# Output projections that end by pairs of token tiles, the next norm's transpositions between their last steps, the first gate diagonal built first, and the odd layer's channel norm two attention units earlier

## Chip, cores and metric

One core of one Trainium2 chip. The metric is the device time of one execution in microseconds (us); lower is better. Three executions of the kernel before gave 1838.09 to 1843.55, median 1841.16.

## What is computed

Two layers of a hybrid trunk over 512 latent tokens and 256 context tokens, width 1024, in float32 precision. Each layer is: norm, mixer, norm and gated residual, norm, gated ConvFFN, norm and gated residual.

```python
for layer in range(2):
    h = rmsnorm(x, g_pre1) * (1 + m[1]) + m[0]          # latent and context
    o = mixer(h)                                        # even: gMLP || GQA; odd: Conformer conv || MLA
    x = x + m[2] * rmsnorm(o, g_post1)
    h = rmsnorm(x, g_pre2) * (1 + m[4]) + m[3]
    x = x + m[5] * rmsnorm(conv_ffn(h), g_post2)        # (silu(dwconv3(z_gate)) * z_up) @ w_out
# conformer_conv: silu(layernorm_over_channels(dwconv31(a * sigmoid(gt))))   -> 512 channels
# mixer output: concat([conv or gMLP branch, attention]) @ w_out (1536 x 1024); conv_ffn's w_out is 2816 x 1024
```

In the last layer only the latent tokens have an output.

## The kernel before, in words

**Numbers in two halves.** Each float32 operand of TensorE is split into a high half (rounded by a ScalarE copy) and a low half (a subtraction on VectorE or GpSimd), and each product is made of three matmuls (high x high, high x low, low x high).

**Weights** arrive as 103 slots of 128 x 2048 (1 MB) through two raw buffers `w_raw`. `round_hi(n)` (ScalarE, L276) makes `w_hi`, `take_lo(n)` (VectorE, L282) makes `w_lo`, and the TensorE waits for the latter in `weights(n)`. The load of a slot waits for the `take_lo` two slots before. The second slot of the odd layer's output projection (`ODO0+1`) is loaded only when attention has ended, because its raw buffer holds attention's `PTo`.

**An output projection** (`out_pe`, four of them: `evo` and `odo` after the mixers with kt = 12 tiles of 128 input channels, `ffo0` and `ffo1` after the ConvFFNs with kt = 22; 6 token tiles in layer 0, 4 in layer 1). For each half h of the 1024 output columns and each input tile k (the step q = h*kt + k) it multiplies all token tiles t into PSUM banks `OUTB[t]`. ScalarE gives the high half of input tile q (`part_hi`, L653), once TensorE is done with the step before the last (`a_used`); VectorE gives the low half (`part_lo`, L659). In steps q = 2, 3 (to 5 with context) TensorE also makes a row of the gate by a product of `ones` with a diagonal matrix `diag` that VectorE builds from the gate column (L752) and copies out (L748), both in `gate_row`. The last 8 input tiles of the second half are run differently: `four(half, t)` is a block of 12 matmuls that multiplies four of them for one token tile, so that the tiles finish one after the other. The order before is f(0,0), f(0,1), f(1,0), f(0,2), f(1,1), and so on, f(1,t) being the one that finishes tile t.

**After a projection**, for each tile t: ScalarE squares (L676), VectorE takes the mean (L758) and the gated copy (L766), GpSimd the power -0.5 (L809), VectorE updates X (L803, `update`). Then the next norm (`pre1`, `pre2` before a ConvFFN or the odd mixer, `pre3` before the last ConvFFN): ScalarE squares X (L704), VectorE takes the mean (L470), GpSimd the power (L499), VectorE multiplies (`pre_xn`, L475; for tiles 2 and 3 of `pre3` ScalarE does, L733), TensorE transposes (L524, steps i = 8g + k: channel tile k of token group g, a group being two token tiles), VectorE applies scale and shift (`pre_affine`, L487), ScalarE makes the high half (`pre_high`, L512), VectorE the low half of even i (L493), GpSimd of odd i (`pre_low`, L505). The first slot after it, `group_slot`, runs its products by token group: each step needs the halves of its own i. In `pre1` and `pre2` the 8 transpositions of group 0 stand around the block f(1, tiles-3); in `pre3` they stand in `group_slot`. Each engine runs in the order in which these instructions are written.

**The odd layer's channel norm** (`cln`) of the Conformer branch lies beside the 32 attention units u of MLA: convolution taps (`conv_steps`, L2029) two a unit until u = CLN-4 = 20, sums on GpSimd, a sum over partitions on TensorE at u = CLN and at CLN+6 (L1852, L1855), the centred squares at CLN+2 and +3 on ScalarE, the first two input tiles of the projection at CLN+4 and +5, and mean and reciprocal at CLN+7 = 31, the last unit (L2173, L2176). The root is taken in step q = 2 of `odo` on ScalarE (L1559), its refinement in q = 4 and 5 on VectorE (L2183 to L2190), the four scaled tiles in q = 5 (L2193), and the SiLU in q = 7 on ScalarE (L1563).

Of the kernel before, what the change touches and what calls it, by code (L numbers as in the profile page):

```python
# [21 lines left out]
ALU = mybir.AluOpType  # L22
# [40 lines left out]
def build(nc, x, ctx, cvec, wpack, modw, modu, modb, normg, ffcw, rope_ev, rope_od, qkg, aln, wsT, bs,  # L63
          odcw, odcln, gcq, gckv, out):
    es = ExitStack()
    with es:
# [411 lines left out]
        def pre_affine(dve, st, layer, which, i0, i1):  # L478

            for i in range(i0, i1):  # L480
                g, k = divmod(i, KD)
                dve.wait_ge(S(st, "tr"), since(st, "tr") + i + 1)
                if i >= 6:
                    dve.wait_ge(S(st, "hi"), since(st, "hi") + i - 5)
                    low = "lo_odd" if i % 2 else "lo_even"
                    dve.wait_ge(S(st, low), since(st, low) + (i - 6) // 2 + 1)
                nc.vector.tensor_scalar(pre_tmps[st][i % 6][:, :], PS[:, pre_bank(st, i), 0:256],  # L487
                                        prescale[:, k, g // 2:g // 2 + 1],
                                        modc[:, layer, 3 * which * KD + k, g // 2:g // 2 + 1], ALU.mult, ALU.add)\
                    .then_inc(S(st, "aff"), 1)  # L490
# [23 lines left out]

        def pre_transposes(pe, st, i0, i1):
# [17 lines left out]
        def group_slot(pe, st, n, groups):  # L533

            ahead, r = PRE_AHEAD[st], n % 2
            last = None
# [34 lines left out]
        PRE_AHEAD = {"pre1": KD, "pre2": KD, "pre3": 0}  # L571

        def out_pe(pe, st, n0, kt, tiles, before=None, norm=None, chunk=None):
# [88 lines left out]
        def slot_turns(kt):  # L662
# [9 lines left out]
        def out_act(act, st, n0, kt, tiles, A, before=None, early=False, beside=lambda q: None):  # L672
# [7 lines left out]
            turns = slot_turns(kt)  # L680
# [19 lines left out]
        def out_then_norm_act(act, square, st, sp, tiles, n_next, mid=lambda: None):  # L700
# [6 lines left out]
            for t in range(tiles - 2):  # L707
                square(t)
                if tiles == NT and t == 3:
                    pre_high(act, sp, 4, KD)  # L710
                    round_hi(act, n_next)
                norm_square(t)
                if tiles == NT and t == 2:
                    pre_high(act, sp, 0, 4)
            if tiles == NT:
                square(4)
# [6 lines left out]
            else:  # L723
                round_hi(act, n_next)
                square(2)
                square(3)
                pre_high(act, sp, 0, 4)
                norm_square(2)
                norm_square(3)
                pre_high(act, sp, 4, KD)  # L730
# [6 lines left out]
        def out_dve(dve, st, n0, kt, tiles, A, layer, which, before=None, chunk=None, early=False, beside=lambda q: None):  # L737
# [32 lines left out]
            turns = slot_turns(kt)  # L770
            for q, (s, j, h, k) in enumerate(out_ktiles(kt)):
                gate_row(q - 2)
# [39 lines left out]
        def out_then_norm_pool(pool, st, sp, tiles):  # L812
            for t in range(tiles - 2):
                out_power(pool, st, t)
                if tiles == NT and t == 2:
                    pre_low(pool, sp, 0, 4)
                pre_power(pool, sp, t)
                if tiles == NT and t == 2:
                    pre_low(pool, sp, 4, KD)
# [1486 lines left out]
```

## Time and profile before

| | |
|---|---|
| median of 3 runs | 1841.16 us |
| profiled execution | 1837.36 us |
| its span, first to last instruction | 1835.6 us |
| mean granted clock of TensorE | 0.989 |
| TensorE busy (matmuls) | 1747.3 us, 95% |
| VectorE, ScalarE, GpSimd busy | 1131.6, 681.2, 182.1 us |

The profile is of one execution. A row of the timeline begins with its start in the span and its duration; in brackets stands how long its engine had been idle before it and who released it. TensorE's matmuls are pipelined, so that one lasts longer than the distance between the starts of two.

### The profile page before, as it was taken

Reading aid. Unit: us, or ns where it says so; the run is one execution under the profiler, and the core shown is the slowest. Engines: PE = TensorE matmul, PEld = TensorE weight load, DVE = VectorE, ACT = ScalarE, POOL = GpSimd, SP = SyncE. Lnnn points to the kernel's source line nnn. Section 1 sums busy time; section 2 is a strip of 40 time slices with the busy share of each in tenths; the row PEclk is TensorE's granted clock in tenths of the full one; section 3 lists DMA queues with packets and bytes.
Section 4 is the critical chain, followed back from the end, with each engine's and each line's share of the span. In section 5 each row is a group of like instructions: output and inputs, shape, how many; then the busy total and the mean of one; then the engine's idle time right before and its main releaser. Section 6 shows DMA issues by size and latency. Waiting matters only on the chain.

```text
span 1835.6 us, 23669 instructions
## 1 busy us (share of the span) xinstructions
PE 1747.3 (95%) x9274; PEld 1468.2 (80%) x9274; DVE 1131.6 (62%) x1692; ACT 681.2 (37%) x1117; POOL 182.1 (10%) x200
## 2 busy tenths in 40 slices
PE   6999999999999999999999999789989899999998
PEld 4777899777888888887777888679977788888776
DVE  5776777687577666545353777877866644443554
ACT  4442366443412212123343433334445423222342
POOL 1176400001100000000000200011210200000000
PEclk9999999999999999999999999899999899999999
DMA  9433000130243444521121132100011132223221
GB/s 363 156 116 114 24 1 1 69 115 23 104 161 137 139 170 158 200 81 69 46 92 46 49 114 71 46 24 1 1 69 69 47 115 91 91 94 110 94 92 69
DMA packets 30994, 166.77 MB, mean 91 GB/s; under 512 B 4144, under 2 KB 4656, under 8 KB 16688
## 3 DMA queue, kind: packets, MB, share of 16 engines
q1 hardware_dynamic: 29024, 163.60, 24.6%
q10 hardware_dynamic: 1872, 1.82, 0.3%
q8 instruction: 67, 1.10, 0.2%
q14 instruction: 31, 0.25, 0.0%
HBM read 163.31 MB, written 2.10 MB: 90 GB/s over the span
## 4 chain that ended last, share of the span: by engine, by line
PE 83%; DVE 7%; issue 4%; ACT 3%; DVEq 1%; DMA 1%; POOL 1%; ACTq 0%; POOLq 0%; SPq 0%
PE PS L293 12%; PE PS L297 12%; PE PS L295 12%; PE PS L583 8%; PE PS L585 7%; PE PS L584 7%; PE PS L1086 5%; PE PS L320 3%; PE PS L322 3%; PE PS L321 3%; PE PS L1071 2%; DVE w_lo L282 2%; ACT w_hi L276 1%; DVE pre_tmp_pre L487 1%; PE PS L597 1%
## 5 line engine op out<-in xcount | busy, mean ns | idle before, releaser
L293 PE MATMUL PS<-HT,w_hi 128*128 128x512 f32 (+1 forms) x1232 | 378.4, 355 | 10.8 <-DVE HT L493 5.0
L297 PE MATMUL PS<-HT,w_lo 128*128 128x512 f32 (+1 forms) x1232 | 370.8, 349 | 0.0
L295 PE MATMUL PS<-HT,w_hi 128*128 128x512 f32 (+1 forms) x1232 | 370.1, 349 | 0.0
L282 DVE TENSOR_TENSOR w_lo<-w_raw,w_hi 128x2048 fp32r<-128x2048 f32 x103 | 237.6, 2308 | 157.2 <-ACT w_hi L276 153.0
L583 PE MATMUL PS<-w_hi,a_ring 128*128 128x512 f32 x680 | 274.5, 404 | 15.1 <-DVE a_ring L659 5.6
L584 PE MATMUL PS<-w_lo,a_ring 128*128 128x512 f32 x680 | 265.8, 391 | 0.0
L293 PEld LDWEIGHTS PS<-HT,w_hi 128*128 128x128 f32 x1232 | 206.9, 189 | 52.3 <-issue 7.0
L276 ACT ACTIVATE w_hi<-w_raw 128x2048 fp32r<-128x2048 f32 x103 | 196.1, 1905 | 136.0 <-PEq L617 69.3
L297 PEld LDWEIGHTS PS<-HT,w_lo 128*128 128x128 f32 x1232 | 206.8, 189 | 30.9
L295 PEld LDWEIGHTS PS<-HT,w_hi 128*128 128x128 f32 x1232 | 206.8, 189 | 30.8
L958 DVE SCALAR_TENSOR_TENSOR yb<-PS,cws,yb 128x511 f32<-128x511 f32 (+1 forms) x132 | 83.2, 658 | 170.0 <-ACTq L924 166.2
L583 PEld LDWEIGHTS PS<-w_hi,a_ring 128*128 128x128 f32 x680 | 128.3, 189 | 56.4 <-issue 24.3
L920 ACT ACTIVATE yb<-PS,cws 128x512 f32<-128x512 f32 x44 | 34.3, 779 | 347.2 <-PE PS L297 347.2
L407 DVE SCALAR_TENSOR_TENSOR m_acc<-m_raw,sT,m_acc 128x1024 f32<-128x1024 f32 x112 | 145.7, 1331 | 26.9 <-DMA m_raw<-modu 22.0
L584 PEld LDWEIGHTS PS<-w_lo,a_ring 128*128 128x128 f32 x680 | 128.2, 189 | 28.9 <-issue 3.4
L585 PE MATMUL PS<-w_hi,a_ring 128*128 128x512 f32 x340 | 133.3, 392 | 0.0
L809 POOL TENSOR_TENSOR rstd<-rstd,halfneg 128x1 f32<-128x1 f32 x20 | 12.6, 629 | 1192.7 <-DVE rstd L758 1192.7
L320 PE MATMUL PS<-w_hi,HT 128*128 128x512 f32 (+1 forms) x272 | 103.8, 381 | 4.3 <-DVE HT L1905 3.1
L322 PE MATMUL PS<-w_hi,HT 128*128 128x512 f32 (+1 forms) x272 | 102.1, 375 | 0.0
L321 PE MATMUL PS<-w_lo,HT 128*128 128x512 f32 (+1 forms) x272 | 102.1, 375 | 0.0
L2029 DVE SCALAR_TENSOR_TENSOR cat_od<-G,ccw,cat_od 128x512 f32<-128x512 f32 x120 | 87.9, 764 | 4.1 <-issue 0.6
L1128 DVE TENSOR_REDUCE rmax<-PS 128x1 f32<-128x768 f32 (+1 forms) x72 | 66.6, 925 | 20.9 <-PE PS L1048 18.3
(307 smaller groups left out, 2603.1 us busy)
## 6 DMA issues: line engine op xcount, KB each, us to landing
w_raw<-wpack SPq DMA_DIRECT2D x103, 1024.0 KB, 4.8
m_raw<-modu SPq DMA_DIRECT2D x80, 512.0 KB, 4.3
mod_raw<-modw SPq DMA_DIRECT2D x8, 1024.0 KB, 12.2
X<-x SPq DMA_DIRECT2D x1, 2048.0 KB, 8.6
out<-X SPq DMA_DIRECT2D x4, 512.0 KB, 2.6
X<-ctx SPq DMA_DIRECT2D x1, 1024.0 KB, 10.8
alnb<-aln ACTq DMA_DIRECT2D x1, 512.0 KB, 4.3
csn<-rope_ev ACTq DMA_DIRECT2D x1, 256.0 KB, 2.6
```

The costliest lines, as they stand in the source:

```text
L276: nc.scalar.activation(w_hi[r][:, :], w_raw[r][:, :], ACT.Copy).then_inc(wh_ready, 1)
L282: nc.vector.tensor_tensor(w_lo[r][:, :], w_raw[r][:, :], w_hi[r][:, :].bitcast(F32), ALU.subtract).then_inc(wl_ready, 1)
L293: nc.tensor.matmul(o, wh, xh, start=start, stop=False)
L295: nc.tensor.matmul(o, wh, xl, start=False, stop=False)
L297: last = nc.tensor.matmul(o, wl, xh, start=False, stop=stop)
L320: nc.tensor.matmul(o, xh, w_hi[r][:, wc], start=k == 0, stop=False)
L321: nc.tensor.matmul(o, xh, w_lo[r][:, wc], start=False, stop=False)
L322: return nc.tensor.matmul(o, xl, w_hi[r][:, wc], start=False, stop=k == KD - 1)
L407: ops.scalar_tensor_tensor(out=acc[g][:, :], in0=raw[:, :], scalar=sT[:, k, g:g + 1], in1=acc[g][:, :], op0=ALU.mult, op1=ALU.add)
L583: nc.tensor.matmul(o, ah, w_hi[n % 2][:, wc], start=k == 0, stop=False)
L584: nc.tensor.matmul(o, ah, w_lo[n % 2][:, wc], start=False, stop=False)
L585: return nc.tensor.matmul(o, al, w_hi[n % 2][:, wc], start=False, stop=k == kt - 1)
```

## The change

Six parts, in the order of the code:

1. The tail of `out_pe` runs by pairs: f(0,0) f(0,1) f(1,0) f(1,1) f(0,2) f(0,3) f(1,2) f(1,3), and with context f(0,4) f(0,5) f(1,4) f(1,5). The four first transpositions of the next norm stand in front of f(1,2), the other four behind it, now for `pre3` too. The sum and the turn of the modulation chunk (in `evo`) stand around f(1,0).
2. ScalarE, VectorE and GpSimd run what follows in the same new order: tiles 0 and 1, group 0's scale and shift between tiles 2 and 3, and so on.
3. For `pre3`, steps 4 to 7 of scale and shift go from VectorE to ScalarE (`pre_affine_high`: an Identity with scale and bias, then the copy to the high half).
4. `gate_row(0)` (the first diagonal) is run at q = 0 instead of q = 2 in all four projections.
5. In `odo`, `round_hi` and `take_lo` of slot ODO0+1 stand at q = 3 instead of q = 1.
6. CLN is 22 instead of 24 (three taps a unit in units 2 to 5); the reciprocal is cut in two halves of 256 columns, in units 29 and 30; the root goes from q = 2 to q = 0, its refinement from q = 4 and 5 to q = 2 and 3, the scaled tiles to q = 3 and 4 (two each), the SiLU from q = 7 to q = 4, 6, 7 (1, 2, 1).

```diff
 def pre_affine(dve, st, layer, which, i0, i1):
     for i in range(i0, i1):
         g, k = divmod(i, KD)
+        if st != "pre3" or not 4 <= i < KD:
...
+def pre_affine_high(act, st, layer, which, i0, i1):
+    for i in range(i0, i1):
+        act.wait_ge(S(st, "tr"), since(st, "tr") + i + 1)
+        if i >= 6:
+            low = "lo_odd" if i % 2 else "lo_even"
+            act.wait_ge(S(st, low), since(st, low) + (i - 6) // 2 + 1)
+        nc.scalar.activation(pre_tmps[st][i % 6][:, :], PS[:, pre_bank(st, i), 0:256], ACT.Identity,
+                             bias=modc[:, layer, 3 * which * KD + i, 0:1], scale=prescale[:, i, 0:1])\
+            .then_inc(S(st, "aff"), 1)
+        act.drain()
+        nc.scalar.activation(HT[:, 0, 0, i, :], pre_tmps[st][i % 6][:, :], ACT.Copy).then_inc(S(st, "hi"), 1)
...
 def group_slot(pe, st, n, groups):
-            if ahead:
-                pe.wait_ge(S(st, "aff"), since(st, "aff") + ahead)
+            if st != "pre3":
+                pe.wait_ge(S(st, "aff"), since(st, "aff") + KD)
...
-                            if g == 0 and k == 0 and ahead == 0:
-                                pre_transposes(pe, st, 0, 3)
-                            if k + 3 < KD and i + 3 >= ahead:
+                            if k + 3 < KD and g:
+                                if g == 1 and k == 0 and st != "pre3":
+                                    pe.wait_ge(S(OUT_OF[st], "o_copy"), since(OUT_OF[st], "o_copy") + NT + 5)
                                 pre_transposes(pe, st, i + 3, i + 4)
...
-            four(0, 0)
-            for t in range(1, tiles):
+            for t in range(0, tiles, 2):
                 four(0, t)
-                if chunk is not None and t == 1:
+                four(0, t + 1)
+                if chunk is not None and t == 0:
                     m_sum(pe, chunk)
-                if chunk is not None and t == 2:
-                    m_turn(pe, chunk)
-                ahead = norm is not None and PRE_AHEAD[norm] and t == tiles - 2
-                if ahead:
+                if norm is not None and t == 2:
                     if chunk is not None:
                         pe.wait_ge(m_evac, chunk + 1)
                     pre_transposes(pe, norm, 0, 4)
-                four(1, t - 1)
-                if ahead:
+                four(1, t)
+                if chunk is not None and t == 0:
+                    m_turn(pe, chunk)
+                if norm is not None and t == 2:
                     pre_transposes(pe, norm, 4, KD)
-            four(1, tiles - 1)
+                four(1, t + 1)
...
-                    at_q[q] = s + 1
+                    at_q[q + 2 if st == "odo" and q == 1 else q] = s + 1
...
             else:                                    # out_then_norm_act, 4 tiles
+                pre_high(act, sp, 0, 1)
                 round_hi(act, n_next)
+                pre_high(act, sp, 1, 4)
                 square(2)
+                pre_affine_high(act, sp, 1, 1, 4, 6)
                 square(3)
-                pre_high(act, sp, 0, 4)
+                pre_affine_high(act, sp, 1, 1, 6, KD)
                 norm_square(2)
                 norm_square(3)
-                pre_high(act, sp, 4, KD)
...
-                gate_row(q - 2)
+                if q == 0:
+                    gate_row(0)
+                elif q >= 3:
+                    gate_row(q - 2)
...
             else:                                    # out_then_norm_dve, 4 tiles
-                pre_xn(dve, sp, 1)
+                affine(0, 4)
                 take_lo(dve, n_next)
-                affine(0, 4)
                 gated(2)
+                affine(4, 6)
                 update(2)
                 gated(3)
                 update(3)
-                affine(4, KD)
+                affine(6, KD)
                 pre_mean(dve, sp, 2)
                 pre_mean(dve, sp, 3)
...
-        CLN = 24
+        CLN = 22
...
-                conv_steps(min(2, 31 * 4 - sum(taps)))
+                conv_steps(min(3 if 2 <= u < 6 else 2, 31 * 4 - sum(taps)))
...
-                    nc.vector.reciprocal(rs_b[:, :], mu[:, :]).then_inc(S("cln", "var"), 1)
+                    nc.vector.reciprocal(rs_b[:, 0:256], mu[:, 0:256])
+                if u == CLN + 8:
+                    nc.vector.reciprocal(rs_b[:, 256:512], mu[:, 256:512]).then_inc(S("cln", "var"), 1)
```

With 4 tiles, tiles 0 and 1 now run as gated(0), update(0), gated(1), update(1), pre_mean(0), pre_mean(1), pre_xn(0), pre_xn(1) on VectorE, and square(0), square(1), norm_square(0), norm_square(1) on ScalarE. GpSimd's powers and low halves follow the same order.

## Rows read from the trace of the kernel before

**Rows 1.** Timeline of TensorE, start of the odd projection (start, us, engine, line).

```profile
1363.94 0.50 PE L583 MATMUL PS<-w_hi,a_ring 128*128 128x512 f32 x1 [0.98 <-DVE mu L2173]
...
1373.19 2.08 PE L597 MATMUL PS<-diag,ones 128*128 128x512 f32 x2 [3.52 <-DVE diag L752]
...
1378.33 1.02 PE L597 MATMUL PS<-diag,ones 128*128 128x512 f32 x2
...
1382.37 0.47 PE L583 MATMUL PS<-w_hi,a_ring 128*128 128x512 f32 x1 [0.26 <-issue]
...
1390.04 0.50 PE L583 MATMUL PS<-w_hi,a_ring 128*128 128x512 f32 x1 [1.94 <-DVE a_ring L659]
```

**Rows 2.** Timeline of VectorE, the same stretch.

```profile
1363.97 3.35 DVE L2176 RECIPROCAL rs_b<-mu 128x512 f32<-128x512 f32 x1
...
1370.06 2.29 DVE L282 TENSOR_TENSOR w_lo<-w_raw,w_hi 128x2048 fp32r<-128x2048 f32 x1 [2.71 <-ACT w_hi L276]
1372.45 0.69 DVE L752 TENSOR_TENSOR diag<-ident,gmcol 128x512 f32<-128x512 f32 x1
...
1379.38 0.69 DVE L748 COPY gmB<-PS 128x512 f32<-128x512 f32 x1 [2.02 <-PE PS L597]
...
1384.69 2.50 DVE L2193 TENSOR_TENSOR cat_od<-cat_od,rs_b 128x512 f32<-128x512 f32 x4
```

**Rows 3.** Timeline of ScalarE, the same stretch.

```profile
1388.14 2.93 ACT L1563 ACTIVATE cat_od<-cat_od,ccln 128x512 f32<-128x512 f32 x4 [0.79 <-PE PS L585]
```

**Rows 4.** Busy time by stretch; the column after POOL is the granted clock.

```profile
1374.00:1376.00 2.00, 2.00 (x5) 1.08 (x4) 0.69 (x1) 0.00 (x0) 0.00 (x0) 0.50 0.89 352
1388.00:1392.00 4.00, 2.06 (x10) 1.61 (x10) 2.18 (x3) 3.57 (x5) 0.00 (x0) 1.00 0.23 82
1454.00:1456.00 2.00, 2.00 (x11) 1.91 (x9) 0.04 (x1) 0.74 (x1) 1.74 (x3) 0.50 0.00 0
1708.00:1710.00 2.00, 2.00 (x6) 1.62 (x5) 1.71 (x3) 0.00 (x0) 0.00 (x0) 0.50 0.93 393
```

**Rows 5.** Timeline of TensorE, from the odd projection's end into the last ConvFFN.

```profile
1442.37 1.09 PE L524 MATMUL PS<-ident,xn_pre 128*128 128x128 f32 x8 [0.89 <-DVE w_lo L282]
...
1452.60 0.58 PE L293 MATMUL PS<-HT,w_hi 128*128 128x256 f32 x1 [4.09 <-DVE HT L493]
...
1458.47 0.38 PE L524 MATMUL PS<-ident,xn_pre 128*128 128x128 f32 x2
...
1468.64 0.49 PE L293 MATMUL PS<-HT,w_hi 128*128 128x512 f32 x1
```

**Rows 6.** Timeline of VectorE, the same stretch.

```profile
1434.81 0.75 DVE L475 TENSOR_SCALAR xn_pre<-X,rstd 128x1024 f32<-128x1024 f32 x1
...
1438.79 0.76 DVE L475 TENSOR_SCALAR xn_pre<-X,rstd 128x1024 f32<-128x1024 f32 x1 [0.66 <-POOL rstd L499]
```

**Rows 7.** Timeline of ScalarE, the same stretch.

```profile
1433.36 0.60 ACT L676 ACTIVATE O_odo<-PS 128x512 f32<-128x512 f32 x1 [1.33 <-PE PS L585]
...
1455.26 2.19 ACT L733 ACTIVATE xn_pre<-X,rstd 128x1024 f32<-128x1024 f32 x2 [1.35 <-POOL rstd L499]
```

**Rows 8.** Timeline of TensorE, end of the first projection.

```profile
442.38 1.07 PE L524 MATMUL PS<-ident,xn_pre 128*128 128x128 f32 x8
443.20 0.48 PE L583 MATMUL PS<-w_hi,a_ring 128*128 128x512 f32 x1
...
446.04 1.04 PE L524 MATMUL PS<-ident,xn_pre 128*128 128x128 f32 x8
```

**Rows 9.** Groups of ScalarE, shapes kept apart (busy us, mean ns).

```profile
L920 ACT ACTIVATE yb<-PS,cws 128x512 f32<-128x512 f32 x44 | 34.3, 779 | 347.2 <-PE PS L297 347.2
...
L512 ACT ACTIVATE HT<-pre_tmp_pre 128x256 fp32r<-128x256 f32 x64 | 26.2, 417 | 26.5 <-DVE pre_tmp_pre L487 25.4
```

**Rows 10.** Timeline of TensorE, start of the last projection.

```profile
1706.69 1.49 PE L597 MATMUL PS<-diag,ones 128*128 128x512 f32 x2 [1.95 <-DVE diag L752]
...
1712.01 1.02 PE L597 MATMUL PS<-diag,ones 128*128 128x512 f32 x2
```

More of the change, by code:

```diff
@@ L481, in pre_affine @@
                 g, k = divmod(i, KD)
[L482 to L490, printed above, removed]
+                if st != "pre3" or not 4 <= i < KD:
+                    dve.wait_ge(S(st, "tr"), since(st, "tr") + i + 1)
+                    if i >= 6:
+                        dve.wait_ge(S(st, "hi"), since(st, "hi") + i - 5)
+                        low = "lo_odd" if i % 2 else "lo_even"
+                        dve.wait_ge(S(st, low), since(st, low) + (i - 6) // 2 + 1)
+                    nc.vector.tensor_scalar(pre_tmps[st][i % 6][:, :], PS[:, pre_bank(st, i), 0:256],
+                                            prescale[:, k, g // 2:g // 2 + 1],
+                                            modc[:, layer, 3 * which * KD + k, g // 2:g // 2 + 1], ALU.mult, ALU.add)\
+                        .then_inc(S(st, "aff"), 1)
                 if i % 2:
@@ L706, in norm_square @@
                 act.drain()
-            for t in range(tiles - 2):
-                square(t)
-                if tiles == NT and t == 3:
-                    pre_high(act, sp, 4, KD)
-                    round_hi(act, n_next)
-                norm_square(t)
-                if tiles == NT and t == 2:
-                    pre_high(act, sp, 0, 4)
-            if tiles == NT:
+            square(0)
+            square(1)
+            norm_square(0)
+            norm_square(1)
+            if tiles == NT:
+                pre_high(act, sp, 0, 4)
+                square(2)
+                pre_high(act, sp, 4, 6)
+                square(3)
+                pre_high(act, sp, 6, KD)
+                norm_square(2)
+                norm_square(3)
+                round_hi(act, n_next)
                 square(4)
@@ L812, in out_then_norm_pool @@
         def out_then_norm_pool(pool, st, sp, tiles):
[L813 to L819, printed above, removed]
+            out_power(pool, st, 0)
+            out_power(pool, st, 1)
+            pre_power(pool, sp, 0)
+            pre_power(pool, sp, 1)
+            pre_low(pool, sp, 0, 4)
+            out_power(pool, st, 2)
+            pre_low(pool, sp, 4, 6)
+            out_power(pool, st, 3)
+            pre_low(pool, sp, 6, KD)
+            pre_power(pool, sp, 2)
+            pre_power(pool, sp, 3)
             if tiles == NT:
@@ L839, in affine @@
                 pre_affine(dve, sp, layer, which, i0, i1)
-            for t in range(tiles - 2):
-                gated(t)
-                if t:
-                    pre_xn(dve, sp, t - 1)
-                update(t)
-                if tiles == NT and t == 2:
-                    affine(0, 4)
-                if tiles == NT and t == 3:
-                    take_lo(dve, n_next)
-                pre_mean(dve, sp, t)
-                if tiles == NT and t == 2:
-                    affine(4, KD)
-            if tiles == NT:
+            gated(0)
+            update(0)
+            gated(1)
+            update(1)
+            pre_mean(dve, sp, 0)
+            pre_mean(dve, sp, 1)
+            pre_xn(dve, sp, 0)
+            pre_xn(dve, sp, 1)
+            if tiles == NT:
+                affine(0, 4)
+                gated(2)
+                affine(4, 6)
+                update(2)
+                gated(3)
+                affine(6, KD)
+                update(3)
+                pre_mean(dve, sp, 2)
+                pre_mean(dve, sp, 3)
+                pre_xn(dve, sp, 2)
+                pre_xn(dve, sp, 3)
+                take_lo(dve, n_next)
                 gated(4)
-                pre_xn(dve, sp, 3)
                 update(4)
@@ L1556, in beside_out @@
             def beside_out(q):
-                if q == 2:
+                if q == 0:
                     act.wait_ge(S("cln", "var"), 2)
                     nc.scalar.activation(nh_b[:, :], rs_b[:, :], ACT.Sqrt).then_inc(S("cln", "rstd"), 1)
-                if q == 7:
-                    for j in range(4):
+                if q in (4, 6, 7):
+                    for j in {4: (0,), 6: (1, 2), 7: (3,)}[q]:
                         act.wait_ge(S("cln", "nrm"), j + 1)
@@ L2191, in beside_out @@
                     dve.drain()
-                    for j in range(4):
+                if q in (3, 4):
+                    for j in range(2 * q - 6, 2 * q - 4):
                         nc.vector.tensor_tensor(cat_od[:, 8 + j, :], cat_od[:, 8 + j, :], rs_b[:, :], ALU.mult)\
```

32 lines of the change are left out of this document (14 added, 18 removed).

## The prediction

> **What bounds the kernel now.** I read first the page's busy shares: TensorE is busy for 95% of the span (the table above), so a change that leaves its products alone can only fill its pauses. I then went through TensorE's timeline for pauses at the four output projections, read for each the engine named as releaser, and last the granted clock by stretch. The pauses are in three places, all in layer 1.
>
> At the start of the odd projection TensorE waits 0.98 us for the variance, 3.52 us for the first diagonal and 1.94 us for a low half at step q = 6 [rows 1]. VectorE shows why: its reciprocal is 3.35 us long and stands behind attention; the diagonal is built only behind `take_lo`, which waited for `w_hi` of the slot loaded after attention; the four scaled tiles (2.50 us) and a `take_lo` stand in front of the low half of q = 6 [rows 2], and ScalarE's four SiLUs (2.93 us) in front of the next one [rows 3]. At its end TensorE waits 0.89 us, then 4.09 us for the low half of channel tile 4 [rows 5]. At the start of the last projection it waits 1.95 us for a diagonal [rows 10]. Behind each of the 3.52, 4.09 and 1.95 us the clock stands at 0.50 of full speed (1.2 of 2.4 GHz); behind the 1.94 us it stays at 1.00 [rows 4]. The second cost is thus half-speed products. The ends of the two layer-0 projections have no such pause: their transpositions are already between blocks, 442.38 to 443.20 for the first four steps [rows 8].
>
> Units of the sum: four transposition steps cost TensorE 0.82 us; a block of 12 products 2.84 us where it follows an interruption (443.20 to 446.04), of which about 0.1 us is its first product, so 2.73 us otherwise [rows 8].
>
> **Start of the odd projection (parts 4, 5, 6).** The sum over partitions at CLN+6 goes from unit 30 to 28; TensorE does it either way. The variance is then ready two units early, so the wait of 0.98 us goes. Against it: at unit 29 VectorE runs a mean (0.7 us) and half the reciprocal (half of 3.35 us, 1.7 us [rows 2]) before it normalises the last unit; by my count of its queue the last transposition of attention waits some 0.3 to 0.5 us longer, but the slow low half that stood there leaves too. I let these cancel: start at 1363.94 - 0.98 = 1363.0.
> Then q = 0 and 1: to 1373.19 less the wait of 3.52 less 0.16 (a pipelined end) is 5.57 us, so 1368.5. The diagonal is long ready. A step with a gate row and its drain is 4.04 us (1378.33 to 1382.37), the drain 0.4 of it [rows 1]: q = 2 3.64, q = 3 4.04, so q = 4 could start at 1376.2.
> VectorE sets that step. Gate row 1 comes out 1.05 us after its product (1378.33 to 1379.38 [rows 1, 2]), at 1369.6; copy and drain 0.76, diagonal 0.6, low half of q = 3 0.6, two refinements 1.3, two scaled tiles 1.25 (half of 2.50), `take_lo` 2.2, second copy 0.6, low half 0.7: 8.0 us, so 1377.6. A new wait of 1.4 us at q = 4. `take_lo` itself is not late for want of weights: its `w_hi` was there at 1370.06 before [rows 2], and ScalarE now makes it after `part_hi` of q = 3, near 1371.4. Then q = 4 and 5, 5.6 us, to 1383.2; at q = 6 ScalarE does two SiLUs (half of 2.93 [rows 3]) and the high half, 0.6, then VectorE the low half, 0.7, behind the end of q = 4: about 0.3 us of wait, so 1383.6 instead of 1390.04. **Gain 6.4 us.** Bounds: without the two new waits 8.1; if the one of 1.4 halves the clock once more, some 1.7 less, 4.7.
>
> **End of the odd projection (parts 1 to 3).** The last block ends at 1442.37 - 0.89 - 0.2 = 1441.3 [rows 5]. In pairs, tile 1 is finished four blocks before that, at 1441.3 - 4 x 2.73 = 1430.4, one block earlier than before. From the square of tile 1 to its `pre_xn` were 5.43 us (1433.36 to 1438.79 [rows 6, 7]); the `pre_xn` of tile 0 that stood in between (0.75 us, at 1434.81 [rows 6]) now stands behind, which lets the update start about 0.5 earlier: 4.95, and 0.76 for the operation. So 1430.6 + 5.7 = 1436.3 against TensorE's 1435.9 (two blocks). TensorE waits 0.5, transposes (0.82), runs f(1,2), transposes, runs f(1,3), and reaches `group_slot` at 1443.7, its first product near 1444.2, about as before (1444.4).
> What follows differs. ScalarE after f(1,2): square 0.8, two pairs of Identity and copy, square of tile 3 after f(1,3), two more pairs. The trace has no Identity of 256 columns from PSUM: below lies the 256-column copy from SBUF, 0.42, above the 512-column Identity from PSUM, 0.78 [rows 9]. I take 0.5 for its length and 1.05 for a pair with its drain. High half 7 is ready at 1446.8. VectorE meanwhile must do `gated(3)` and `update(3)` before the low half of step 6: 1447.9. TensorE needs 0.36 us a step, reaches step 6 at 1446.4 and waits 1.5. Then two squares of X (2.5 us) and two scalings (2.19 [rows 7]) put group 1's transpositions at 1451.6, where TensorE waits a second time, 1.2 us. Before they were at 1458.47. From there the 10.17 us to the next slot (to 1468.64 [rows 5]) are paced by VectorE's and ScalarE's work on 8 tiles, which is the same. **Gain 6.8 us.** Bounds: a pair at 1.5 us and half clock (1.7) over the second group leave 3.5; pairs at 0.9 and no waits give 8.
> The Trainium skill (ScalarE: Activation LUTs, Rules for kernel authors) speaks against this step: cheap arithmetic belongs on VectorE. By the same page's costs (What ACT_TABLE_LOAD costs) an activation with two pointer operands would be 0.58 us for 256 columns, an estimate; the gain here would be 6.5. No row here shows the operation.
>
> **Start of the last projection (part 4).** VectorE's diagonal moves from behind `take_lo` to in front of it. TensorE needs that `take_lo` too at q = 2, so only drain and diagonal, 0.85 us, go from the 1.95: 1.1 us of wait stays. Between the two gate rows lie 5.32 us (1706.69 to 1712.01 [rows 10]) against 3.64 at full clock; if the shorter pause leaves the clock up, 1.7 us more. **Gain 2.5 us**, at least 0.85.
>
> **Ends of the two layer-0 projections (parts 1, 2).** The new order gives TensorE nothing there, and the transpositions come two blocks (5.46 us) after tile 1, with the same chain of 5.9 us as above: a wait of 0.5 to 0.6 us each. In the first, the turn of the modulation chunk moves forward by one block and so does what waits for it, so the distance is the same. Everything later (the next slot's `take_lo`, group 0's halves) is ready by my count at least 1 us before TensorE comes. **Loss 1.2 us**; bounds 0 and 3 (1.5 each, if the chain is a microsecond longer). The new wait for `o_copy` stands behind a gated copy that is long done.
>
> **Neutral.** One tap more in units 2 to 5: VectorE idles over 0.7 us in each of these units, TensorE is full.
>
> Sum: 6.4 + 6.8 + 2.5 - 1.2 = 14.5 us, the profiled execution from 1837.4 to 1822.9. The median of before is 3.8 above its profiled time; I carry the difference over: 1841.2 - 14.5 = **1826.7 us**.
>
> **Rivals.**
> *Half clock at the new waits.* For it: 1.95 us of pause was enough [rows 4]. Against: 1.94 us was not, and the new ones are 1.1 to 1.5 us. If it falls at q = 4 and at step 6 and stays down in the last projection: gain 14.5 - 1.7 - 1.7 - 1.7 = 9.4, 1831.8 us. Chance 0.22. The Trainium skill (TensorE: Matmul & The Clock Gate, Why this matters for your kernels) says that only longer pauses between bursts cost the clock; by that the drop behind 1.95 us would not be due to that pause and would stay, while q = 4 and step 6 would be harmless: 1828.4, inside the range.
> *ScalarE becomes the bound in `pre3`.* It takes four Identities besides all its squares; if a pair costs 1.5, gain 10.5 to 11.5, 1830. Chance 0.12.
> *The odd start gives nothing.* If `take_lo` of the second slot at q = 3 comes 3 us later than I count, TensorE pauses 4.4 us at q = 4 with the clock halved behind it, and the diagonal's wait has only moved: that place gives 2 and the rest 3, some 1836 to 1838. Chance 0.10.
> *Slower.* The transpositions now stand in front of f(1,2) in three projections, and TensorE is in order. If `pre_xn` of tile 1 were 5 us later than I count, each place would stop TensorE for 5.5 us with half clock behind it, 7 each, 21 in all against 15.7 of gains: 1846. It decides from 3.5 us a place. The chain before, 5.43 us with one operation more in it [rows 6, 7], speaks against. Chance 0.04.
> *Forecast* 0.52.
>
> **Range and chances.** 1820 to 1834: gains from 7 to 17.3, with the spread of the runs (2 to 3 us) on the fast side. A measurement tells 0.3%, 5.5 us, from no change: faster 0.86, same 0.09, slower 0.05 (all but the last two cases are faster).
>
> **What would show it.** In the trace after: no wait at the first gate row of the odd projection, one of about 1.4 us at q = 4, q = 6 about 20.6 us behind the first product (26.1 before); in the last ConvFFN's first slot waits for a low half and for ScalarE's scaled X instead of one of 4.09; a wait of 0.5 us in front of L524 three times; 0.50 clock in none of the stretches of rows 4. I am wrong if the clock falls at the new waits, if ScalarE's pairs are longer, or if TensorE stops anywhere in layer 0 for over a microsecond.

## The result and the profile after

The changed kernel took 1828.07 us in the median of 4 runs (1827.35 to 1829.13), the one before 1840.24 in the median of 4 (1838.09 to 1843.55): ratio 0.9933, 95% interval 0.9916 to 0.9950. Its profiled execution took 1827.39 us (span 1825.6, mean granted clock 0.992) against 1837.36 before. The interval leaves out 1, so the changed kernel is faster, by 0.7%. The forecast was 1826.7 in 1820 to 1834, faster with 0.86.

Where the 10.0 us between the two profiled executions come from, by TensorE's rows:

| stretch | before | after | difference | forecast |
|---|---|---|---|---|
| start to the first projection's tail | | | +0.5 | 0 |
| tails of the two layer-0 projections | 37.55, 35.18 | 38.34, 36.09 | +1.7 | +1.2 |
| last attention units, to the first odd product | 39.81 | 39.65 | -0.2 | -0.98 |
| first odd product to q = 6 | 26.10 | 20.73 | -5.4 | -5.4 |
| q = 6 to the second slot of the ConvFFN | 78.60 | 74.21 | -4.4 | -6.8 |
| last projection, first product to second gate row | 13.00 | 10.51 | -2.5 | -2.5 |
| rest | | | +0.2 | 0 |

(First row: the step in front of the tail begins at 418.10 and 418.57. The third row runs from the transpositions at 1324.13, after 1326.69.)

The rows from the second to the sixth, which hold the places that the change was made for, add up, before rounding, to 10.7 us of gain.

Timeline of TensorE after, from the last attention units to the last projection; the rows answer to [rows 1, 5, 10]:

```profile
1331.34 1.13 PE L1879 MATMUL PS<-mu,ones 128*128 128x512 f32 x2 [0.71 <-DVE KNl L2182]
...
1366.34 0.48 PE L596 MATMUL PS<-w_hi,a_ring 128*128 128x512 f32 x1
...
1371.90 1.02 PE L610 MATMUL PS<-diag,ones 128*128 128x512 f32 x2
...
1381.03 0.47 PE L596 MATMUL PS<-w_hi,a_ring 128*128 128x512 f32 x1 [1.72 <-DVE a_ring L671]
...
1387.07 0.50 PE L596 MATMUL PS<-w_hi,a_ring 128*128 128x512 f32 x1 [0.32 <-DVE a_ring L671]
...
1433.85 1.09 PE L538 MATMUL PS<-ident,xn_pre 128*128 128x128 f32 x8 [0.80 <-DVE xn_pre L475]
...
1446.92 0.39 PE L293 MATMUL PS<-HT,w_hi 128*128 128x256 f32 x1 [2.84 <-DVE HT L494]
...
1450.85 0.58 PE L538 MATMUL PS<-ident,xn_pre 128*128 128x128 f32 x2
...
1461.28 0.48 PE L293 MATMUL PS<-HT,w_hi 128*128 128x512 f32 x1
...
1698.43 1.12 PE L610 MATMUL PS<-diag,ones 128*128 128x512 f32 x2 [1.08 <-DVE w_lo L282]
...
1702.14 1.02 PE L610 MATMUL PS<-diag,ones 128*128 128x512 f32 x2
```

The waits of 0.98, 3.52 and 4.09 us are gone, the one of 1.94 us is 0.32. In their place stand 0.71 (first channel sum, not foreseen), 1.72 (q = 4), 0.80 (transpositions) and 2.84 us (step 6), and in layer 0 a wait of 0.89 and one of 0.80 us in front of the transpositions. The first gate row has no wait; the last projection's is 1.08 us.

Busy time by stretch after (the column after POOL is the granted clock), to set beside [rows 4]:

```profile
1380.00:1384.00 4.00, 2.97 (x13) 2.49 (x14) 4.00 (x6) 2.10 (x2) 0.00 (x0) 1.00 0.71 262
1446.00:1450.00 4.00, 3.08 (x18) 3.08 (x19) 1.08 (x4) 3.34 (x4) 1.10 (x2) 0.73 0.00 0
1698.00:1702.00 4.00, 3.57 (x14) 2.64 (x15) 3.31 (x6) 1.82 (x2) 0.00 (x0) 1.00 0.58 203
```

The clock stays at full speed around q = 4 and in the last projection, and falls behind the 2.84 us at step 6.

VectorE after, end of the odd projection, and GpSimd beside it:

```profile
1437.77 0.75 DVE L494 TENSOR_TENSOR HT<-pre_tmp_pre,HT 128x256 fp32r<-128x256 f32 x1 [1.08 <-ACT HT L513]
1438.45 2.82 DVE L282 TENSOR_TENSOR w_lo<-w_raw,w_hi 128x2048 fp32r<-128x2048 f32 x1
...
1442.24 1.76 DVE L824 SCALAR_TENSOR_TENSOR X<-O_both_odo,rstd,X 128x1024 f32<-128x1024 f32 x1
...
1444.83 1.70 DVE L824 SCALAR_TENSOR_TENSOR X<-O_both_odo,rstd,X 128x1024 f32<-128x1024 f32 x1
1446.45 0.41 DVE L494 TENSOR_TENSOR HT<-pre_tmp_pre,HT 128x256 fp32r<-128x256 f32 x1
```

```profile
1437.51 1.61 POOL L506 TENSOR_TENSOR HT<-pre_tmp_pre,HT 128x256 fp32r<-128x256 f32 x2 [4.50 <-ACT HT L513]
...
1441.99 0.93 POOL L506 TENSOR_TENSOR HT<-pre_tmp_pre,HT 128x256 fp32r<-128x256 f32 x1
...
1444.72 0.72 POOL L506 TENSOR_TENSOR HT<-pre_tmp_pre,HT 128x256 fp32r<-128x256 f32 x1
```

The low half of step 6, for which TensorE waits, stands behind `update(3)`. Four VectorE operations in its queue are longer than their like elsewhere (`take_lo` 2.82 against 2.29 us [rows 2], the updates 1.76 and 1.70 against 1.29 for tile 1, the low half of step 2 0.75 against 0.41 for that of step 6), and in front of each a subtraction of GpSimd had begun.

### The profile page after: what moved, and what is told of

Same layout as the page of the kernel before. It is cut to its first block, busy times and chain, and to the rows that moved or that the text cites. A ratio compares the mean times of both kernels' runs of the same rounds, so it can differ in the third digit from the quotient of the medians.

```text
span 1825.6 us, 23680 instructions
## 1 busy us (share of the span) xinstructions
PE 1743.4 (95%) x9274; PEld 1464.9 (80%) x9274; DVE 1131.3 (62%) x1689; ACT 683.4 (37%) x1121; POOL 187.5 (10%) x200
## 4 chain that ended last, share of the span: by engine, by line
PE 83%; DVE 7%; issue 4%; ACT 3%; DVEq 1%; POOL 1%; DMA 0%; ACTq 0%; POOLq 0%; SPq 0%
PE PS L293 12%; PE PS L297 12%; PE PS L295 12%; PE PS L596 7%; PE PS L598 7%; PE PS L597 7%; PE PS L1113 5%; PE PS L320 3%; PE PS L322 3%; PE PS L321 3%; PE PS L1098 2%; DVE w_lo L282 2%; DVE pre_tmp_pre L488 1%; ACT w_hi L276 1%; PE PS L1071 1%
```

## Experiments

All times below are of one profiled execution each unless a ratio is given. A place is judged by its own stretch, because the start of the odd projection shifts by up to 6 us between executions of one kernel (see the last section).

**e1: part 4 alone.** Kernel before with

```diff
-                gate_row(q - 2)
+                if q == 0:
+                    gate_row(0)
+                elif q >= 3:
+                    gate_row(q - 2)
```

> Kernel before with part 4 alone (first diagonal at q = 0). Theory: the last projection gains 2.5 us as in the full change (a pause of about 1.1 instead of 1.95 us and full clock behind it), the two layer-0 projections nothing, and the odd start about 1 us: the pause of 3.52 us only moves one place on, since the low half of q = 2 still stands behind the take_lo of slot ODO0+1 (ready at 1372.35), so the products of q = 2 begin near 1373 instead of 1374.2. Profiled time 1837.4 - 3.5 = 1833.9. Rival: the diagonal alone was what TensorE waited for; then the odd start gives 3.5 + 1.7 and the profiled time is 1829.7.

TensorE of e1:

```profile
1378.09 0.50 PE L583 MATMUL PS<-w_hi,a_ring 128*128 128x512 f32 x1 [2.78 <-DVE a_ring L659]
```

The wait of 3.52 us for the diagonal became one of 2.78 us for the low half of q = 2, with half clock behind it. First odd product to q = 6: 25.58 us instead of 26.10. The last projection has the full 2.5 us (10.51). The theory holds, with 0.5 us at the odd start instead of 1: the diagonal was not what had to move, the `take_lo` in front of the low half was. (Profiled time 1838.53 where 1833.9 was forecast. Its first odd product begins 4.7 us late, at 1368.67; in front of it TensorE's clock stood at half for 30.7 us in all, in the kernel before for 20.5.)

**e2: parts 4 and 5.** e1 and

```diff
-                    at_q[q] = s + 1
+                    at_q[q + 2 if st == "odo" and q == 1 else q] = s + 1
```

> Kernel before with parts 4 and 5 (diagonal at q = 0, second slot's round_hi and take_lo at q = 3), the channel norm where it was. Theory: the odd projection's pauses are all gone except the 0.98 us for the variance: VectorE's queue behind the reciprocal (ends 1367.3) is 0.7 + 0.7 us until the low half of q = 2 at 1368.7, before TensorE comes at 1369.5; the refinement and the scaled tiles are done by 1381.5 and q = 6 starts near 1383, 19 to 20 us behind the first product instead of 26.1. With 2.5 of the last projection the gain is 9 to 9.5 us, profiled 1828, which is more than parts 4 to 6 together give. Rival: part 6 is what clears q = 4 to 6; without it the scaled tiles and a pause of 2 us stay in front of q = 6, the gain is 6 us or less, 1831.5 or more.

VectorE and TensorE of e2:

```profile
1384.13 2.50 DVE L2196 TENSOR_TENSOR cat_od<-cat_od,rs_b 128x512 f32<-128x512 f32 x4
1386.55 2.28 DVE L282 TENSOR_TENSOR w_lo<-w_raw,w_hi 128x2048 fp32r<-128x2048 f32 x1
1388.75 0.68 DVE L659 TENSOR_TENSOR a_ring<-cat_od,a_ring 128x512 fp32r<-128x512 f32 x1
```

```profile
1389.48 0.50 PE L583 MATMUL PS<-w_hi,a_ring 128*128 128x512 f32 x1 [1.95 <-DVE a_ring L659]
```

First odd product to q = 6: 21.30 us. No pause is left before q = 6, as forecast, but the scaled tiles and a `take_lo` (which I had left out of the count at q = 5) still stand in front of its low half: a wait of 1.95 us, and half clock behind it, 1.6 us more. With the last projection the gain by the stretches is 4.8 - 1.6 + 2.5 = 5.7 us; the ratio is 0.9962 (0.9949 to 0.9975), that is 7.0 us (4.6 to 9.4), which doesn't tell theory and rival apart. The place itself does. So part 5 gives 4.3 of the 5.4 us in this stretch (25.58 to 21.30), and part 6 another 0.6, and with it the half clock goes. My theory that part 6 costs more than it gives fell, and the rival holds: part 6 is what clears q = 6. In whole times the worth of part 6 doesn't show clearly: e3's ratio of 0.9953 lies within e2's interval.

**e3: parts 4, 5 and 6.** e2 and the whole of part 6.

> Kernel before with parts 4, 5 and 6, projection tails as before. Theory: the start of the odd projection and of the last one as in the changed kernel: q = 6 20.7 us behind the first product, with pauses of 1.7 us at q = 4 and 0.3 at q = 6, minus about 0.7 us for the new wait of the first channel sum: 5.5 + 2.5 = 8 us of gain, profiled 1829.4. Rival: the tail's parts and the starts interact (clock, buffers); then this and the tail alone do not add up to the 10 us of the full change within 1 us.

20.73 us from the first odd product to q = 6, waits of 1.72 and 0.32 us, 0.71 at the channel sum, 10.50 us in the last projection: 8.1 us by the stretches, ratio 0.9953 (0.9938 to 0.9967). The projection tails are as before (37.52 and 35.12 us; 78.52 from q = 6 to the slot).

**e4: parts 1 to 3.** The kernel before with the tails and all that follows them, and nothing of parts 4 to 6.

> Kernel before with parts 1 to 3 alone (order of the tails, transpositions between the blocks, ScalarE's four steps). Theory: the end of the odd projection gains 4.4 us (from its step q = 6 to the next slot 74.2 instead of 78.6 us), the ends of the layer-0 projections lose 0.8 to 0.9 us each: 2.7 us in all, profiled 1834.7, which the 0.3% of this measurement hardly tells from no change. Rival, my prediction's own terms: 6.8 - 1.2 = 5.6 us, 1831.8.

Ratio 0.9980 (0.9967 to 0.9994). The layer-0 tails take 38.37 and 36.12 us, 1.8 more than before; from q = 6 to the next slot 75.80 us, of which 1.6 are half clock behind a pause that was there before too (the wait at q = 6), so 74.2 without it. By these stretches the theory holds; the interval of the ratio, 1.1 to 6.1 us of gain, has room for both theory and rival. The parts add up within the intervals: 0.9953 x 0.9980 = 0.9933.

**e5: part 3 undone.** Changed kernel with

```diff
-                if st != "pre3" or not 4 <= i < KD:
+                if True:
...
-                pre_affine_high(act, sp, 1, 1, 4, 6)
+                pre_high(act, sp, 4, 6)
...
-                pre_affine_high(act, sp, 1, 1, 6, KD)
+                pre_high(act, sp, 6, KD)
```

> Changed kernel with part 3 undone: VectorE does the scale and shift of steps 4 to 7 of the last ConvFFN's norm again. Theory (the Identity on ScalarE is worth having since VectorE's queue is what TensorE waits for there): four operations of 0.5 us, 2.0 us in all, go into VectorE's queue between take_lo and the low half of step 6, so step 6 starts about 2.0 us later and group 1's transpositions with it; from q = 6 of the odd projection to the next slot 76.2 us instead of 74.2. Rival, the rule that cheap arithmetic belongs on VectorE: ScalarE's two squares and two scalings, freed of 4 x 0.57 us, come that much earlier and the interval is 74.2 or less.

```profile
1445.36 0.39 PE L293 MATMUL PS<-HT,w_hi 128*128 128x256 f32 x1 [1.16 <-POOL HT L506]
...
1448.54 0.58 PE L293 MATMUL PS<-HT,w_hi 128*128 128x256 f32 x1 [2.57 <-DVE HT L494]
```

```profile
1447.62 0.87 ACT L513 ACTIVATE HT<-pre_tmp_pre 128x256 fp32r<-128x256 f32 x2 [3.52 <-DVE pre_tmp_pre L488]
1448.39 1.04 ACT L716 ACTIVATE xn_pre<-X 128x1024 f32<-128x1024 f32 x1
```

From q = 6 to the next slot 76.84 us instead of 74.21: part 3 is worth 2.6 us. TensorE waits at steps 5 and 6 (1.16 and 2.57 us); step 6 starts 1.4 us later than in the changed kernel, where 2.0 were forecast. ScalarE's squares come later, not earlier: in its queue they stand behind the high halves of steps 6 and 7, which wait 3.52 us for VectorE's scale and shift, and that stands behind `update(3)`. So the scaled tile 3 is ready 65.8 us behind q = 6 instead of 62.9. The clock was at half for longer here than in the changed kernel's trace (6.8 us instead of 3.4), but TensorE came to group 1 only 0.3 us after that tile, so the 2.6 us are hardly due to it.

**e6: the low halves of steps 5 and 7 on VectorE.** Changed kernel; GpSimd's `pre_low` leaves them out and VectorE's `pre_affine` has

```diff
+                    if st == "pre3" and i in (5, 7):
+                        dve.wait_ge(S(st, "hi"), since(st, "hi") + i + 1)
+                        dve.wait_ge(S(st, "lo_odd"), since(st, "lo_odd") + i // 2)
+                        nc.vector.tensor_tensor(HT[:, g, 1, k, :], pre_tmps[st][i % 6][:, :],
+                                                HT[:, g, 0, k, :].bitcast(F32), ALU.subtract)\
+                            .then_inc(S(st, "lo_odd"), 1)
```

> Changed kernel with the low halves of steps 5 and 7 of group 0 on VectorE instead of GpSimd, so that no GpSimd operation of 128x256 lies beside update(2) and update(3). Theory (GpSimd's operations slow VectorE's that run beside them): the two updates last 1.28 us instead of 1.76 and 1.70, while the two extra subtractions cost VectorE 0.34 us each; step 6 starts about as before, within 0.3 us. Rival (the updates are long because of what they read or write here): they stay at 1.7 us and step 6 starts 0.7 us later.

```profile
1443.52 1.27 DVE L832 SCALAR_TENSOR_TENSOR X<-O_both_odo,rstd,X 128x1024 f32<-128x1024 f32 x1
...
1445.62 1.28 DVE L832 SCALAR_TENSOR_TENSOR X<-O_both_odo,rstd,X 128x1024 f32<-128x1024 f32 x1
```

The updates are 1.27 and 1.28 us long: GpSimd's subtractions were what lengthened them. Step 6 starts 59.29 us behind q = 6 instead of 59.85, 0.56 earlier where at most 0.3 was forecast, and the whole stretch is 73.59 instead of 74.21 us: the same work done by VectorE alone is faster there than shared with GpSimd.

**e7: scaling before the second mean, and CLN = 23.** Changed kernel with

```diff
             pre_mean(dve, sp, 0)
-            pre_mean(dve, sp, 1)
             pre_xn(dve, sp, 0)
+            pre_mean(dve, sp, 1)
             pre_xn(dve, sp, 1)
...
-        CLN = 22
+        CLN = 23
```

> Changed kernel with two edits at separate places. (a) VectorE runs pre_mean(0), pre_xn(0), pre_mean(1), pre_xn(1) instead of both means first: theory, the scaling of tile 0 leaves the end of the chain, the scaling of tile 1 starts about 0.35 us earlier, and TensorE's wait in front of the transpositions falls from 0.89, 0.80 and 0.80 to about 0.5 us at the three places; rival: the second mean comes late behind the scaling (it waits for GpSimd's power) and the wait grows to over 1.1 us. (b) CLN = 23: theory, the wait of 0.71 us of the first channel sum for the last piece of the keys goes, and the second half of the reciprocal (1.74 us) stands one unit later, which costs less than that: from the first transposition wait of the attention's last units nothing new, the first odd product 0.3 to 0.7 us earlier in its stretch. Rival: the reciprocal holds the root and then q = 2 to 4, and the pause of 1.72 us at q = 4 grows by 0.5 us or more.

```profile
440.29 1.07 PE L538 MATMUL PS<-ident,xn_pre 128*128 128x128 f32 x8 [0.62 <-DVE xn_pre L475]
...
1447.82 0.39 PE L293 MATMUL PS<-HT,w_hi 128*128 128x256 f32 x1 [2.83 <-DVE HT L494]
1450.94 0.44 PE L538 MATMUL PS<-ident,xn_pre 128*128 128x128 f32 x2 [0.34 <-ACT xn_pre L751]
```

(a) The three waits are 0.62, 0.53 and 0.54 us instead of 0.89, 0.80 and 0.80: 0.27 each. (b) The wait of 0.71 us at the sum is gone, and the waits in the last two units are 0.4 us shorter; from the transpositions at 1326.69 (1329.43 in e7) to the first odd product it takes 38.06 us instead of 39.65, 1.6 us less, where 0.3 to 0.7 were forecast; of that some 0.5 us stands in no row that I can name. The pause at q = 4 stays at 1.72. In this execution the clock also stayed up behind the pause at step 6, and the stretch from q = 6 was 72.99 us.

**e8: the low half of step 6 in front of `update(3)`.** Changed kernel with

```diff
                 gated(3)
-                update(3)
                 affine(6, KD)
+                update(3)
```

> Changed kernel with the low half of step 6 in front of update(3) on VectorE. Theory (the chain over update(3), the square, the power and ScalarE's two scalings bounds group 1): TensorE's wait at step 6 falls from 2.84 to 1.0 to 1.2 us and the clock stays up behind it, but group 1's transpositions then wait about 3 us for the scaled tile 3, which comes at 1450.0 + 0.35; the interval from q = 6 to the next slot stays at 74.2 within 0.5 us. Rival (the low half of step 6 is the bound): the interval falls by 1.7 us of wait and up to 1.5 us of half clock, to 71 to 72.5.

```profile
1450.21 0.39 PE L293 MATMUL PS<-HT,w_hi 128*128 128x256 f32 x1 [1.03 <-DVE HT L494]
...
1455.34 0.44 PE L538 MATMUL PS<-ident,xn_pre 128*128 128x128 f32 x2 [2.12 <-ACT xn_pre L751]
```

1.03 us at step 6, then 2.12 us for ScalarE's scaled tile (about 3 were forecast), and the stretch is 74.55 us instead of 74.21. The scaled tile 3 is ready 63.1 us behind q = 6, in the changed kernel 62.9. The pause only moved, as the theory had it: the bound is the chain over `update(3)`. The half clock moved with it, from behind step 6 to behind the 2.12 us.

**e9: the combination.** Changed kernel with e6, e7 and

```diff
-                affine(0, 4)
+                affine(0, 3)
+                pre_affine(dve, sp, layer, which, 3, 4, low=False)
                 take_lo(dve, n_next)
+                dve.wait_ge(S(sp, "hi"), since(sp, "hi") + 3)
+                nc.vector.tensor_tensor(HT[:, 0, 1, 2, :], pre_tmps[sp][2][:, :], HT[:, 0, 0, 2, :].bitcast(F32),
+                                        ALU.subtract).then_inc(S(sp, "lo_even"), 1)
...
-                for t in (2, 3):
+                for t in (2,):
                     act.wait_ge(S(sp, "rstd"), since(sp, "rstd") + t + 1)
...
                 pre_mean(dve, sp, 3)
+                pre_xn(dve, sp, 3)
...
-                if q in (3, 4):
-                    for j in range(2 * q - 6, 2 * q - 4):
+                if q in (3, 4, 5):
+                    for j in {3: (0,), 4: (1, 2), 5: (3,)}[q]:
```

> Changed kernel with all that helped and what follows from it: the order of e7 and CLN = 23, the low halves of steps 5 and 7 on VectorE (e6), and three edits not run before: the scaling of tile 3 on VectorE beside that of tile 2 on ScalarE; take_lo of the last ConvFFN's first slot in front of the low half of step 2, so that it starts when w_hi is ready, some 0.9 us earlier; the four scaled tiles of the channel norm at q = 3, 4, 4, 5 instead of 3, 3, 4, 4. Theory (VectorE's queue from take_lo to the scaling of tile 3 is what bounds the odd projection's end): from q = 6 to the next slot 73.0 us less 0.6 (e6), 0.8 and 0.9, some 70.7; the pause at q = 4 falls from 1.72 to 1.2 us; the stretch before the first odd product 1.6 us shorter than in the changed kernel; in all 5.5 to 6 us less than the changed kernel, a profiled time near 1821.5. Rival (by then ScalarE's squares or TensorE's own products bound the end): the edits do not add up, and the interval stays at 72.4 or more, the whole at 3.5 us less.

TensorE, VectorE and GpSimd of e9:

```profile
1379.23 0.47 PE L604 MATMUL PS<-w_hi,a_ring 128*128 128x512 f32 x1 [1.33 <-DVE a_ring L679]
...
1443.36 0.39 PE L293 MATMUL PS<-HT,w_hi 128*128 128x256 f32 x1 [1.34 <-DVE HT L494]
```

```profile
1435.10 2.29 DVE L282 TENSOR_TENSOR w_lo<-w_raw,w_hi 128x2048 fp32r<-128x2048 f32 x1 [0.47 <-ACT w_hi L276]
1437.31 0.96 DVE L905 TENSOR_TENSOR HT<-pre_tmp_pre,HT 128x256 fp32r<-128x256 f32 x1
```

```profile
1435.45 3.42 POOL L514 TENSOR_TENSOR HT<-pre_tmp_pre,HT 128x256 fp32r<-128x256 f32 x2 [4.50 <-ACT HT L521]
```

Ratio to the kernel before 0.9902 (0.9885 to 0.9918), median 1825.08 us (1822.66 to 1825.53) beside 1830.68 for the changed kernel on the same chip, without overlap. From q = 6 to the next slot 71.12 us (70.7 expected), no wait left for group 1's transpositions, no half clock in the odd projection; 38.07 us before the first odd product, 20.32 from there to q = 6, where 0.4 of the 0.5 us expected at q = 4 came. The edits add up. `take_lo` now begins before GpSimd's two subtractions and is back at 2.29 us, and they take 3.42 us instead of 1.61. The low half behind it (L905) started when the second of them was under way, and takes 0.96 us. The two profiled executions, 1822.66 and e10's 1833.29 us, differ by 10.6 us and the medians by 5.6; the last section says where a part of this comes from.

**e10: the changed kernel again.**

> The changed kernel itself beside the one before, so that the combination can be compared with it on the same chip. Theory: 10 to 12 us faster than before (ratio 0.9935), the profiled intervals as in its first trace: 20.7 us from the first odd product to q = 6, 74.2 from there to the next slot (73.0 if the clock stays up behind the pause at step 6), 10.5 to the second gate row of the last projection. Rival: the first result was a lucky clock; then the ratio is above 0.996.

Ratio 0.9929 (0.9912 to 0.9947); 20.73, 74.23 and, in the last projection, 1.08 us of wait at the gate row with full clock. The first result stands.

## Why the prediction was right, step by step

**The number came nearer than its sum.** A gain of 14.5 us was forecast. The places that it was made of gave 10.7, the two profiled executions differ by 10.0 and the medians by 12.2. The profiled execution was forecast at 1822.9 us and took 1827.39. The median still came within 1.4 us of 1826.7, because I had added the 3.8 us by which the profiled execution of before lay under its median, and for the changed kernel this distance was only 0.7 us. That was luck. Of the missing 4.5 us, 2.4 belong to the end of the odd projection, 0.8 to its start, 0.5 to the layer-0 tails, and about 0.7 to stretches where nothing was forecast.

**Start of the odd projection: right.** q = 6 was forecast at 20.6 us behind the first product and came at 20.73; the new waits at 1.4 and 0.3 us and came at 1.72 and 0.32. VectorE's sum of 8.0 us held: q = 4 starts 14.7 us behind the first product, forecast 14.6; the wait is longer because TensorE was there 0.2 us earlier. e1 and e2 show the mechanism: part 5 carries 4.3 us, the diagonal 0.5. The step "start at 1363.94 - 0.98" was mis-sized: moving the norm two units forward puts the first channel sum in the unit whose PSUM bank VectorE has not yet read (0.71 us, `KNl`, L2182), and 0.2 of the 0.98 us is left as gain. e7 shows it: one unit later the sum costs nothing, and 1.6 us come back.

**End of the odd projection: right in kind, 2.4 us too large.** Forecast 6.8, measured 4.4. The step that failed is the low half of step 6: TensorE was to wait 1.5 us for it and waited 2.84. Counted from q = 6, the low half was forecast at 57.9 us and was ready at 59.8, while TensorE came at 57.0 instead of 56.4. The delay lies in VectorE's queue: beside GpSimd's subtractions `take_lo` and the two updates are 0.53, 0.48 and 0.42 us longer, 1.4 us in all, and the low half of step 2 is 0.3 us longer. The recorded sum doesn't list the terms of this queue, but it names no such lengthening. e6 takes the two updates back to 1.28 us and e9 `take_lo` to 2.29. Two smaller things add to it: the wait at the transpositions was 0.3 us longer than forecast, and behind the 2.84 us the clock fell. Group 1's transpositions, forecast 61.6 us behind q = 6, came at 63.8. The wait of 1.2 us for the scaled tile 3 didn't show, since that tile was ready at 62.9, before TensorE came at half clock; in e7, with the clock up, it is a wait of 0.34 us. ScalarE's Identity is 0.57 and 0.55 us, where I took 0.5 and the Trainium skill (ScalarE: Activation LUTs, What ACT_TABLE_LOAD costs) leads to an estimate of 0.58; the pair is 0.97 us, not 1.05. The Trainium skill's rule that cheap arithmetic belongs on VectorE (same page, Rules for kernel authors) doesn't hold where VectorE's queue is what TensorE waits for: by e5 it would cost 2.6 us here.

**Last projection: right,** 2.5 us, 1.08 us of wait left, clock up. e1 has all of it with part 4 alone. e4 shows a grain of luck in it: there the old pause of 1.96 us stood with the clock up behind it, and the stretch took 11.39 us. Of the 2.5 us, 0.9 are the shorter wait and the rest is a half clock that the old pause brings in some executions.

**Layer-0 tails: right in kind, 0.5 us too small.** 1.7 us lost (0.8 and 0.9) against 1.2; the wait is 0.89 and 0.80 us. The chain is 0.3 us longer than counted: both means stand in front of the first scaling, and the second scaling waits for it (e7).

**Rivals.** The half clock came at step 6 and not at q = 4 nor in the last projection; only part of that rival. By its own list of signs the prediction was wrong there, since the clock fell at a new wait. The 1828.4 us that it gives under its first rival lies nearest to the measured median, but not for the reason given there: in the last projection the clock stayed up, and at step 6 it fell. ScalarE was not the bound of group 0. The diagonal's wait did move in e1, but not with part 5 in. Nothing stopped TensorE for over a microsecond in layer 0 at the tails.

## What to carry to other kernels

A wait names its last releaser; the thing to move is what stands in front of that releaser in its queue. Here the diagonal was named and a `take_lo` was the price (e1 against e2), and the low half of step 6 was named while the chain over an update was the price (e8). Before an operation is shared out between VectorE and GpSimd, look at who starts first: here, on the queue that bounded the stretch, the subtractions were cheaper on VectorE itself (e6). When a stage is moved forward by units, check for each unit which buffer its first instruction takes over.

## What the runs showed of the hardware that I had not expected

**VectorE and GpSimd block each other by order of start.** Where GpSimd's subtraction started first, VectorE's operation that followed was longer (`update` 1.76 and 1.70 against 1.28 us, `take_lo` 2.82 against 2.29; in e9 a low half 0.96 against 0.42). Where VectorE started first, it kept its length and GpSimd's grew: e9's pair 3.42 against 1.61 us. In e5 a subtraction, 0.73 us long where it runs alone, was issued 0.16 us behind an update and took 1.71:

```profile
1443.44 1.28 DVE L824 SCALAR_TENSOR_TENSOR X<-O_both_odo,rstd,X 128x1024 f32<-128x1024 f32 x1
```

```profile
1443.60 1.71 POOL L506 TENSOR_TENSOR HT<-pre_tmp_pre,HT 128x256 fp32r<-128x256 f32 x1 [1.40 <-ACT HT L513]
```

The Trainium skill (SBUF — State Buffer, Who interferes with whom) says that the order of issue decides who blocks, and the traces agree.

**A pause of 1.9 to 3.3 us costs the clock in some executions and not in others.** Full pauses of TensorE in the 12 traces of this case, and in how many of them the clock went to half behind or in the pause:

| pause, us | where | to half | stays up |
|---|---|---|---|
| 3.79 to 7.69 | three in every trace, between 1165 and 1232 us | 36 | 0 |
| 3.44 to 5.23 | the odd projection's two ends | 6 | 0 |
| 3.18 to 3.22 | near 220 us, every trace | 11 | 1 (e4) |
| 2.54 to 3.62 | near 27 us, every trace | 5 | 7 (up to 3.23 us) |
| 2.12 to 2.87 | the odd projection, changed kernel and e1, e4 to e8, e10 | 7 | 1 (e7) |
| 2.27 to 2.30 | near 1120 us, every trace | 7 | 5 |
| 2.06 to 2.07 | start of the second layer-0 projection, every trace | 4 | 8 |
| 1.94 to 1.96 | q = 6 and the last projection's gate row | 3 | 3 |
| 1.56 to 1.73 | four places | 0 | all |

Shorter pauses, standing alone, never had it fall (the last 10 us of the span left out). In the kernel before, two pauses of 0.89 us only 2 us apart (1442.37 and 1444.36) had it at half from 1444.4 us on; the same two in e1, e2 and e3 did not. Three of these cases, by stretch (the column after POOL is the granted clock):

```profile
1446.00:1450.00 4.00, 2.18 (x18) 2.18 (x19) 1.99 (x4) 2.60 (x6) 1.45 (x3) 1.00 0.10 41
1450.00:1454.00 4.00, 3.62 (x29) 3.08 (x28) 2.50 (x6) 2.27 (x5) 0.73 (x1) 1.00 0.00 0
```

is e7 behind 2.83 us, and

```profile
1392.00:1396.00 4.00, 4.00 (x15) 3.16 (x14) 0.69 (x1) 0.63 (x1) 0.00 (x0) 0.73 0.24 100
```

e2 behind 1.95 us; e4, behind the 3.20 us near 220 us, has

```profile
222.00:226.00 4.00, 3.68 (x30) 3.55 (x31) 3.05 (x6) 1.57 (x3) 4.00 (x3) 1.00 0.09 37
```

The Trainium skill (TensorE: Matmul & The Clock Gate, Why this matters for your kernels) has only longer pauses cost the clock; the measurements here decide otherwise. What tells the one case from the other stayed open. A fall costs 1.6 us where TensorE is busy behind it (e2 against e3 from q = 6 to q = 16: 31.00 and 29.41), and nothing where another wait follows: behind the 2.06 us, from the first product to the first gate row it takes 10.43 us with the clock up (the kernel before, with a wait of 1.47 us in it) and 10.45 at half clock (the changed kernel, without that wait). Most pauses of that length are thus worth something beyond their own duration in some executions, and this is a part of why executions of one kernel differ: the changed kernel's own runs beside e9 went from 1827.75 to 1833.36 us. In e10, 1833.29 us, the odd projection began 5.8 us later than in the first trace of the same kernel, and in front of it the clock was at half for 34.1 us instead of 23.9; 10.2 us more at half clock are about 5.1 us of TensorE's work, an estimate.
